# Two transposes set inside product groups and two weighted sums set behind the next group, in a three-layer transformer kernel

## What is computed

```
def hybrid_mixer(x, w_in, w_branch_sb, w_branch_moba, w_out):
    proj = x @ w_in
    q_sb, k_sb, v_sb, q_mb, k_mb, v_mb, g_sb, g_mb = jnp.split(proj, cuts, axis=-1)
    o_sb = stick_breaking_attention(heads(q_sb), heads(k_sb), heads(v_sb))
    o_mb = moba_attention(partial_rope(heads(q_mb), pos), partial_rope(heads(k_mb), pos), heads(v_mb))
    branch_sb = merge_heads(o_sb) @ w_branch_sb
    branch_mb = merge_heads(o_mb) @ w_branch_moba
    merged = jax.nn.sigmoid(g_sb) * branch_sb + jax.nn.sigmoid(g_mb) * branch_mb
    return merged @ w_out

for l in range(2):
    x = layer_norm_2(ALPHA * x + hybrid_mixer(x, ...), g, b)
    x = layer_norm_2(ALPHA * x + (silu(x @ w_gate) * (x @ w_up)) @ w_down, g, b)
```

## Time and profile before

| | us |
|---|---|
| median of 3 runs | 1626.96 |
| lowest and highest run | 1625.04, 1627.74 |
| the profiled execution, its whole time | 1625.33 |
| its span in the trace | 1623.5 |
| TensorE busy | 1593.5 (98%) |
| DVE, ACT busy | 856.2 (53%), 612.3 (38%) |

### The profile page before, as it was taken

How to read it: one execution, slowest core, us unless ns; L and a number is a source line. 1 busy time by engine, 2 the same in 40 slices (tenths; PEclk the granted TensorE clock), 3 DMA queues, 4 the chain that set the end, 5 groups by cost and what they waited for, 6 DMA issues and landing times.

```text
span 1623.5 us, 22250 instructions
## 1 busy us (share of the span) xinstructions
PE 1593.5 (98%) x9341; PEld 1151.9 (71%) x9342; DVE 856.2 (53%) x1192; ACT 612.3 (38%) x827; POOL 27.8 (2%) x48
## 2 busy tenths in 40 slices
PE   7999999999999999999999999999999999999998
PEld 5965567874444444444458877899998877799997
DVE  3668776653222222222245866864546685875544
ACT  3414553321111111111134766553433666553431
POOL 0200010000000000000000000000000000000000
PEclk9999999999999999999999999999999999999999
DMA  9877763669999999999993435464545444564540
GB/s 387 233 228 265 303 239 115 251 254 378 422 421 420 421 421 421 421 421 421 421 376 130 164 128 208 156 206 158 196 142 207 156 156 141 170 226 164 191 146 27
DMA packets 129875, 418.55 MB, mean 258 GB/s; under 512 B 6976, under 2 KB 54224, under 8 KB 98864
## 3 DMA queue, kind: packets, MB, share of 16 engines
q1 hardware_dynamic: 107488, 271.15, 45.3%
q10 hardware_dynamic: 17568, 127.93, 18.9%
q0 software_dynamic: 4720, 18.03, 3.9%
HBM read 416.04 MB, written 2.95 MB: 258 GB/s over the span
## 4 chain that ended last, share of the span: by engine, by line
PE 91%; DVE 5%; DMA 2%; ACT 2%; issue 1%; SPq 0%; DVEq 0%
PE bank L982 21%; PE bank L1380 14%; PE bank L1698 13%; PE bank L1393 7%; PE bank L1648 6%; PE bank L1342 4%; PE bank L1171 4%; PE bank L1403 4%; PE bank L930 4%; PE bank L997 3%; PE bank L1669 2%; DMA weight_ring<-in_w_ada 1%; PE bank L964 1%; DVE ring_low L2621 1%; PE bank L1296 1%; PE bank L1553 1%
## 5 line engine op out<-in xcount | busy, mean ns | idle before, releaser
L2621 DVE TENSOR_TENSOR ring_low<-weight_ring,high_ring 128x2048 fp32r<-128x2048 f32 x92 | 208.1, 2288 | 54.8 <-ACT high_ring L1909 54.4
L1380 PE MATMUL bank<-weight_ring,arena 128*64 128x512 f32 x768 | 225.1, 592 | 0.0
L982 PE MATMUL bank<-high_ring,split 128*128 128x512 f32 x608 | 195.7, 396 | 0.0
L982 PE MATMUL bank<-ring_low,split 128*128 128x512 f32 x464 | 180.6, 397 | 0.0
L1909 ACT ACTIVATE high_ring<-weight_ring 128x2048 fp32r<-128x2048 f32 x92 | 172.2, 1905 | 10.5 <-PE bank L982 5.9
L1380 PEld LDWEIGHTS bank<-weight_ring,arena 128*64 128x64 f32 x768 | 71.8, 137 | 145.9 <-issue 145.9
L1698 PE MATMUL bank<-split,ring_low 128*128 128x256 f32 x576 | 162.6, 282 | 0.0
L1698 PE MATMUL bank<-split,high_ring 128*128 128x256 f32 x832 | 148.9, 280 | 0.0
L982 PEld LDWEIGHTS bank<-high_ring,split 128*128 128x128 f32 x608 | 114.1, 188 | 31.0 <-issue 3.2
L1698 PEld LDWEIGHTS bank<-split,high_ring 128*128 128x128 f32 x832 | 128.7, 189 | 0.7
L1393 PE MATMUL bank<-weight_ring,arena 128*64 128x512 f32 x384 | 116.8, 598 | 0.6 <-DVE arena L2563 0.6
(11 more groups left out here) (342 smaller groups left out, 2902.3 us busy)
## 6 DMA issues: line engine op xcount, KB each, us to landing
weight_ring<-in_w_in SPq DMA_DIRECT2D x62, 1024.0 KB, 8.4
weight_ring<-in_w_e_gate SPq DMA_DIRECT2D x49, 1024.0 KB, 9.3
weight_ring<-in_w_e_up ACTq DMA_DIRECT2D x46, 1024.0 KB, 14.4
weight_ring<-in_w_e_down ACTq DMA_DIRECT2D x46, 1024.0 KB, 14.3
weight_ring<-in_w_ada SPq DMA_DIRECT2D x24, 1024.0 KB, 11.0
weight_ring<-in_w_ffn_gate SPq DMA_DIRECT2D x22, 1024.0 KB, 5.4
weight_ring<-in_w_ffn_up SPq DMA_DIRECT2D x22, 1024.0 KB, 7.9
weight_ring<-in_w_ffn_down SPq DMA_DIRECT2D x22, 1024.0 KB, 5.3
```

Source lines behind the costliest of these rows:

```text
L982: last = mm(bank(key)[:, :], left[a_][:, n, t * P:(t + 1) * P], wv[b_][:, j, :], start=(n == 0 and i == 0), stop=(n == kts * len(units_) - ...
L1380: last = mm(hidden_bank[side * CAP:(side + 1) * CAP, :].rearrange("p (j n) -> p j n", n=FF), xgT[:, p // 2 % 2, kt, at:at + CAP], hidden_u ...
L2621: V.tensor_tensor(lower(key), ring[:, units.place[key][0], :], upper(key, layer), ALU.subtract)\
```

## The change

Four things are moved on TensorE, in each of the two layers; DVE, ACT, SP and POOL keep their lists.

- `kmT` 1 is no longer turned behind `kmT` 0, but in the middle of filler 7, between its two weight units.
- `weighted_sum(2)` stands behind filler 8 instead of in front of it.
- `weighted_sum(5)` stands behind the first `bs` group instead of in front of it.
- `normed_turn(1)` stands in the middle of `hidden_rows(1, 0)`, between `fg` and `fu`, instead of in front of it.

```
-                    if p:
+                    if p and p != NS:
                         weighted_sum(p - 1)
                     filler(FILLERS_OF_STEP[p][0])
+                    if p == NS:
+                        weighted_sum(p - 1)
                     if p == NS - 1:
                         pe.wait_ge(sem("roped"), 2 * TT * (layer + 1))
-                        for which, name in enumerate(("qmT", "kmT")):
-                            for t in range(TT):
-                                turns((name, t), [qk[:, which, t, j * P:(j + 1) * P] for j in range(4)], layer)
+                        for which, name, t in ((0, "qmT", 0), (0, "qmT", 1), (1, "kmT", 0)):
+                            turns((name, t), [qk[:, which, t, j * P:(j + 1) * P] for j in range(4)], layer)
...
                     for i in FILLERS_OF_STEP[p][1:]:
-                        filler(i)
+                        filler(i, last_keys_turn if p == NS - 1 else None)
...
                 sums_turn(1)
-                weighted_sum(2 * NS - 1)
...
                             if (b, t, n) == (0, 0, 0):
+                                weighted_sum(2 * NS - 1)
                                 sums_spread(1)
...
                 hidden_rows(0, 0)
-                normed_turn(1)
-                hidden_rows(1, 0)
+                hidden_rows(1, 0, lambda: normed_turn(1))
```

More of the change, by code:

```diff
@@ L1570, in sums_spread, with filler, last_keys_turn @@
                     full(mm(bank(("spread", t))[:, :], k("pair")[0:2, :], inverse[0:2, :], start=True, stop=True), ("spread", t))
-                def filler(i):
+                def filler(i, between=None):
                     name, n, t = FILLERS[i]
-                    token_split((name, n, t), xs, t, both(("l_in", name, n)), 4, layer)
+                    token_split((name, n, t), xs, t, both(("l_in", name, n)), 4, layer, between)
+                def last_keys_turn():
+                    turns(("kmT", 1), [qk[:, 1, 1, j * P:(j + 1) * P] for j in range(4)], layer)
                 for p in range(2 * NS):
```

## The result

| | before | changed |
|---|---|---|
| median, us | 1626.1 (4 runs, 1625.04 to 1627.74) | 1638.8 (4 runs, 1636.65 to 1639.32) |
| span of the profiled execution, us | 1623.5 | 1637.3 |

The changed kernel is slower: the ratio is 1.0075, with a 95% interval from 1.0063 to 1.0087, or +12.7 us. The forecast was +6.9 us, 1633.9 us, in a range from 1629.0 to 1637.0; the result lies above it. The sign was right and the size was about half of what came.

A forecast was written before the change was run, and what follows sets the result against it. TensorE, busy 98% of the span, was taken as the bound. Place costs 2 x 2.07 + 2 x 0.6 + 0.9 + 0.7 = 6.9 us slower gave 1633.9 us against the median; 8-in-10 range 1629.0 to 1637.0 us.

The forecast's parts named there:

- The bank 5 wait of 1.15 us: Before filler 7: its bank holds `qmT` 1 until DVE reads it out, so 0.56 us of wait becomes 1.15 us.
- the 2.34 us for side 1: TensorE's wait before turning side 1 of the stick weights, whose ACT and DVE chain moves 3.44 us; forecast 2.35 us.
- the freed `weighted_sum(2)`: Set behind filler 8, this sum finds its data ready, so its wait of 0.83 us goes.
- This place costs 2.07 us: Turn of `kmT` 1 with `weighted_sum(2)`, each layer: idle 1.15 + 2.35 against 0.56 + 0.83 us, the rest rounding.
- the wait of 2.35 us: TensorE, done with filler 7 and side 0's turn, waits from 946.72 to 949.07 for side 1.
- the right rival: The clock: a new long wait slows the products behind it, 1.5 us a layer, 1636.9 us in all; chance 5%.
- waits of up to 1.06 us show no such loss: Argument against the clock loss: waits of that length in the middle of the program show none.
- the 24 products at the start: Behind the 9.14 us starting idle: 195 ns each against 133 ns, giving the clock loss as 1.5 us a layer.
- Forecast +0.6 us a layer: `weighted_sum(5)`: its 0.45 us wait goes, but ACT's delay makes TensorE wait about 1.0 us before `merged_turn(0)`.
- Forecast +0.9 and +0.7 us: `normed_turn(1)`, layers 0 and 1: `hidden_rows(0, 1)` waits about 1.8 us for DVE to free bank 2.
- a failed cover: First place: moved work other engines should still finish in time, such as filler 8's low part; failure adds up to 1 us.
- the clock at 3 us for both layers: Clock loss of 1.5 us once per layer, giving 1636.9 us, within the range's upper end; chance 5%.

The follow-up runs named there:

- keys_late_read: `keys_alone` with ACT's copy of `kmT` 1 moved behind both exps and DVE's low part behind side 1 of the stick weights; 1624.53 us, ratio 0.9992.
- all_busy: Changed kernel plus two spare products into the free bank of side 1, in the gap before its turn; 1635.74 us, ratio 1.0055.
- all_busy_twice: `all_busy` plus two more spare products into bank 1 in the 1.98 us gap before `hidden_rows(0, 1)`; 1633.66 us, ratio 1.0045.
- normed_bank: `normed_alone` with `fg` 2 in bank 1 and `fg` 3 in bank 2; 1623.86 us, ratio 0.9984 against the kernel before.
- sum5_act_first: Kernel before with only `weighted_sum(5)` moved, and ACT doing the two `bm` high parts ahead of `values_out(5)`; 1625.32 us, ratio 0.9997.
- three_mended: Kernel before with the three moves other than `kmT` 1, plus the ACT reorder and the bank change; 1621.24 us, ratio 0.9971.
- normed_alone: Kernel before with only `normed_turn(1)` moved between the halves of `hidden_rows(1, 0)`; 1630.11 us, ratio 1.0029.
- keys_alone: Kernel before with only the turn of `kmT` 1 moved into the middle of filler 7; 1637.31 us, ratio 1.0067.
- four_mended: `three_mended` plus the move of `kmT` 1 with its late readers as in `keys_late_read`; 1621.81 us, ratio 0.9974.
- sum2_alone: Kernel before with only `weighted_sum(2)` moved behind filler 8; 1624.96 us, ratio 0.9993.

## Why the prediction was right in sign and wrong in size

**The turn of `kmT` 1: the waits right, their price wrong.** The bank 5 wait of 1.15 us, the 2.34 us for side 1 and the freed `weighted_sum(2)` came as worked out, and `keys_late_read` shows that the chain behind the turn is the reason. The step that failed is the term "This place costs 2.07 us": it counted the waits alone and put the clock behind them at nothing, so TensorE was to go on at full rate behind the wait of 2.35 us. The waits cost 2.2 us in each layer, but the lower clock behind them added 1.7 and 3.3 us, and the place cost 3.9 and 5.5 us.

**The clock: the right rival, thrown out on too thin a ground.** It was given 5% and 1.5 us a layer. Its ground against was that "waits of up to 1.06 us show no such loss", which says nothing of 2.3 us, and the trace of before held no wait above 1.3 us behind the start. The size came from the 24 products at the start, and these rows don't measure a fall of the clock: the granted clock is 1.00 there too (10 to 12 us, trace of before), and in the trace of the changed kernel the same 24 products took 5.49 us in place of 4.67. What slowed them is open; the clock's price behind the gap was 1.7 us and 3.3 us. `all_busy` and `all_busy_twice` show that the gap is what the fall hangs on: behind 2.34 us left empty the clock fell in four cases of four, behind the same gap filled in none of four, and with every wait for data in place 4.9 of the 12.7 us went. With the clock's measured 5.0 us in its sum the forecast would have been 1638.9 us. The Trainium skill, page "TensorE: Matmul & The Clock Gate", section "HAM oscillation", was cited for that rival: in the case told there the clock falls to half in waits for DMA of about 3 to 5 us between bursts of products. The traces here agree in kind, at 0.50 behind gaps of 2.34 us and in some cases of 1.98 us, but these gaps are shorter than the waits of that case, so the citation did not by itself make this rival's result follow, as the prediction says it does.

**`weighted_sum(5)`.** Forecast +0.6 us a layer, measured +0.3 and +0.4 us by the traces. The wait of 0.99 us is as forecast. What was too high is the time of the release. The forecast let the first `bs` group start at 992.65, when the turn in front of it ends; it started 0.24 us ahead of that end in the record (998.65 against 998.29 + 0.60), since neighbouring products overlap. So `values_out(5)` moved by 2.3 us in place of 2.5 (994.23 to 1002.75 - 6.23 = 996.52), and DVE took up `low` of `l_wo` 0,0 0.3 us later in place of 0.57 (1007.98 to 1014.52 - 6.23 = 1008.29).

**`normed_turn(1)`.** Forecast +0.9 and +0.7 us, measured +0.8 and +0.6 us. The bank was the cause, as `normed_bank` shows. The wait was 1.98 us where 1.8 was forecast: TensorE was ready 0.3 us sooner than in the sum (1061.78 - 6.55 = 1055.23 against 1055.5) and went on 0.1 us sooner (1063.76 - 6.55 = 1057.21 against 1057.3).

**The whole.** Between the two traces lie 13.8 us against 6.9 us of the forecast. The difference is 5.0 us of clock behind the gaps and 2.3 us in code that the change doesn't touch (1.7 us of clock at 216 us, 0.65 us at the start), less 0.4 us of waits.

**The range.** Its upper end, 1637.0, allowed for one mishap, a failed cover or the clock at 3 us for both layers. The clock took 5.0 us. Its price hangs on the largest new wait of the forecast and should have been set beside it: whoever forecasts a wait longer than any in the trace is outside what the trace can say about the engine behind it.

## What to carry to other kernels

An instruction that waits is often itself what others wait for: before other work is put in front of it, follow its readers in the lists of the other engines, and the bank of the work that moves up. If they have no slack, move the readers too (`keys_late_read`, `sum5_act_first`) or change the bank (`normed_bank`); in `three_mended` three of the moves then pay their full 4.6 us. The fourth, `kmT` 1, pays nothing beside them: its wait of 0.56 us only turns into one of 1.15 us for bank 5. And price a new gap of TensorE at more than its length: 2.34 us of idle cost 4.0 and 5.6 us here (2.34 + 1.7, 2.34 + 3.3). Two spare products into a free bank kept the clock up behind that gap, but in one layer it then fell behind the next long gap, until that was filled too.

## What was not expected of the hardware

- **Equal gaps, unequal effects.** The 1.98 us gap was followed by the lower clock in one of two layers in `normed_alone`, in the other layer in `all_busy`, and in none in the changed kernel. The 2.34 us gap was followed by it in all four cases seen (two layers, two kernels), for 3.4 us in one and for 6.6 to 7 us in the other three. Behind the gaps of 0.99 to 1.16 us in the two layers it was not seen. What decides between equal gaps is open; no run here set out to tell. The two kinds of gap differ in more than their length: the 2.34 us stand between two turns of four transposes, the 1.98 us between product groups.
- **A clock that falls in untouched code.** In the traces of the changed kernel, `keys_alone`, `all_busy`, `normed_bank` and `four_mended` TensorE ran at the lower level for some 3.4 us from about 216 or 217 us on, in `normed_alone` and `all_busy_twice` from about 269 or 270 to 273 us, and in the other six traces, that of before among them, at neither. The instructions there are the same in all of them, so 1.7 us of the 13.8 us between the two traces are this. Part of the 3 us by which the runs of one kernel scatter goes with the clock too: in each of the three sessions the runs of before with a mean granted clock of 0.999 average about 1625.2 us, and those with 0.998 about 1626.4 us. That these 1.2 us come from stretches of this kind, of 1.7 us each, is not shown, since each kernel has one trace. With such a scatter eleven runs did not show in the median the gain of 1.7 us that a trace shows plainly (`sum2_alone`).
